# Eight modulation groups of the second block's odd layer are summed up on VectorE under the first feed forward, and GpSimd spreads the reciprocals of the attentions

## The reference

```python
x = x + concat(y_diff, y_moba) @ w_out[i]
x = x + conv_ffn(rms_norm(x, ln_ffn_g[i]), w_up[i], conv_w[i], conv_b[i], w_down[i])
```

```python
for i in range(2):
    ml = split(silu(c) @ w_ada[i] + b_ada[i], 6)        # latents
    mc = split(silu(c_ctx) @ w_ada[i] + b_ada[i], 6)    # context
    u_lat = rms_norm(h_lat, g_pre_mix[i]) * (1 + ml[1]) + ml[0]     # u_ctx likewise with mc
    o_lat, o_ctx = mixer(u_lat, u_ctx)                  # o_ctx in layer 0 only
    h_lat = h_lat + ml[2] * rms_norm(o_lat, g_post_mix[i])
    f_lat = square(relu(modulate(h_lat, g_pre_ff[i], ml[3], ml[4]) @ w_ff1[i])) @ w_ff2[i]
    h_lat = h_lat + ml[5] * rms_norm(f_lat, g_post_ff[i])
return h_lat
```

## Time and profile before

| | |
|---|---|
| median of three runs | 1936.65 us |
| profiled execution | 1936.78 us, span 1934.9 us |
| TensorE busy (matmul) | 1869.8 us, 97% |
| VectorE busy | 1105.8 us, 57% |
| ScalarE busy | 861.6 us, 45% |
| GpSimd busy | 211.9 us, 11% |
| bytes moved by DMA | 264.68 MB, 137 GB/s |

### The profile page before, as it was taken

The page is one execution under the profiler, slowest core; times in us unless marked ns, Lnnn a source line. Parts: engine busy times, 40 slices in busy tenths (PEclk is TensorE's granted clock), DMA queues, the critical chain, the costliest instruction groups (busy, mean ns, idle before and its releaser), DMA issues. The chain is left out here.

```text
span 1934.9 us, 37112 instructions
## 1 busy us (share of the span) xinstructions
PE 1869.8 (97%) x15824; PEld 1559.3 (81%) x15824; DVE 1105.8 (57%) x1835; ACT 861.6 (45%) x1559; POOL 211.9 (11%) x249
## 2 busy tenths in 40 slices
PE   7999999999999999999999999999999999899998
PEld 5768998776899788756898888888887798579986
DVE  6566774566667554476557665444444565546643
ACT  5465653446656542465322335322222254655532
POOL 2101221110122100103122211000000011000000
PEclk9999999999999999999999999999999999899999
DMA  7777665467766541353000042333332234024653
GB/s 267 250 256 224 189 183 175 166 227 263 223 166 195 175 142 55 115 174 110 26 4 4 4 151 65 104 119 98 100 107 88 66 99 139 25 88 133 194 180 124
DMA packets 219354, 264.68 MB, mean 137 GB/s; under 512 B 14214, under 2 KB 153782, under 8 KB 214711
## 3 DMA queue, kind: packets, MB, share of 16 engines
q1 hardware_dynamic: 218603, 261.49, 42.4%
q10 hardware_dynamic: 588, 0.82, 0.1%
HBM read 261.20 MB, written 1.09 MB: 136 GB/s over the span
## 5 line engine op out<-in xcount | busy, mean ns | idle before, releaser
L404 PE MATMUL acc<-rounded,rounded 128*128 128x512 f32 (+1 forms) x2552 | 875.1, 343 | 9.6 <-DVE rounded L684 4.1
L405 PE MATMUL acc<-rounded,rounded 128*128 128x512 f32 (+1 forms) x2552 | 867.0, 340 | 0.0
L406 PE MATMUL acc<-rounded,rounded 128*128 128x512 f32 (+1 forms) x2552 | 866.8, 340 | 0.0
L388 DVE TENSOR_TENSOR rounded<-arena,rounded 128x2048 fp32r<-128x2048 f32 (+1 forms) x194 | 434.3, 2241 | 285.9 <-ACT rounded L377 285.8
L404 PEld LDWEIGHTS acc<-rounded,rounded 128*128 128x128 f32 x2552 | 480.6, 188 | 80.1 <-issue 14.7
L405 PEld LDWEIGHTS acc<-rounded,rounded 128*128 128x128 f32 x2552 | 480.7, 188 | 60.0 <-issue 1.9
L406 PEld LDWEIGHTS acc<-rounded,rounded 128*128 128x128 f32 x2552 | 480.5, 188 | 60.0
L377 ACT ACTIVATE rounded<-arena 128x2048 fp32r<-128x2048 f32 (+1 forms) x194 | 362.9, 1873 | 341.6 <-PE acc L406 296.4
L1624 DVE SCALAR_TENSOR_TENSOR arena<-acc,pcol,arena 128x254 f32<-128x254 f32 (+1 forms) x176 | 76.8, 478 | 52.3 <-ACT arena L1605 50.8
L2200 PE MATMUL sc<-arena 64*64 64x64 f32 x2560 | 94.7, 221 | 8.8 <-DVE arena L2350 7.7
L2764 ACT ACTIVATE arena<-acc 128x512 f32<-128x512 f32 (+1 forms) x64 | 31.4, 490 | 159.6 <-PE acc L406 159.6
(11 more groups left out here) (265 smaller groups left out, 1691.6 us busy)
## 6 DMA issues: line engine op xcount, KB each, us to landing
arena<-in_w_ff SPq DMA_DIRECT2D x64, 1024.0 KB, 5.4
arena<-in_w_ada SPq DMA_DIRECT2D x48, 1024.0 KB, 5.1
arena<-in_w_up SPq DMA_DIRECT2D x88, 512.0 KB, 5.1
arena<-in_w_in SPq DMA_DIRECT2D x24, 1024.0 KB, 5.3
arena<-in_w_down SPq DMA_DIRECT2D x20, 1024.0 KB, 5.0
arena<-in_w_out SPq DMA_DIRECT2D x16, 1024.0 KB, 5.1
arena<-in_w_in_even SPq DMA_DIRECT2D x9, 1024.0 KB, 5.3
arena<-in_w_in_odd SPq DMA_DIRECT2D x8, 1024.0 KB, 5.2
```

The lines of the kernel that those rows point to most:

```text
L388: dve.tensor_tensor(r32(w), w, r32(high_slot(c)[:, 0:size(c)]), ALU.subtract).then_inc(split_made, 1)
L404: pe.matmul(ps, ah, bh, start=first, stop=False)
L405: pe.matmul(ps, ah, bl, start=False, stop=False)
L406: return pe.matmul(ps, al, bh, start=False, stop=last)
```

## The change

The eight groups leave the two attentions. Their 16 chunks stand in the list ahead of each `ff1(e)` and each `ff2(e)` (`plan_late`), so that the order in the first feed forward is one added chunk, two product chunks, one added chunk, and so on. `late_dve`, called ahead of the split of the chunk two positions on, adds up the 128x512 parts of an added chunk on VectorE, each multiplied by its column of silu(c), into `late_sum`; `late_pe` adds over the partitions by four matmuls with ones in the middle of the next `ff1` (the last one in the last round of `ff2`), and `late_add` adds the bias. The gains and gates of the odd layer follow at the start of `proj1` instead of scan step 0, except the gain of its first norm, and are transposed and stored apart from those of layer 0.

In the 48 units "by feature", GpSimd writes the broadcast reciprocals to SBUF (`widen`), and TensorE turns them by one transpose in place of the two matmuls. In `attBc` GpSimd's eight products stand between the units' copies.

Definitions that go away are shown by their first line (their text stands above). Not shown are the places of the new buffers, `ada_gains` (layer 0 alone now), the gates' loads and the calls of `widen` in the other attentions.

```diff
                 release.append((acc_full, acc_at[key] + i + 1))
-        ada_chunk = {}
-        def plan_ada(blocks, fill_of):
...
+        late_read = sem("late_read")
+        late_chunk = []
+        def plan_late():
+            n = len(late_chunk)
+            view = I["w_ada_2"][1].rearrange("(k p) n -> p k n", p=P)
+            c, k0 = 512 * (4 + n // 2), 4 * (n % 2)
+            late_chunk.append(len(chunks))
+            whole.add(len(chunks))
+            chunks.append(view[:, k0:k0 + 4, c:c + 512])
+            release.append((late_read, n + 1))
+            if n % 2:
+                stage(("late", n // 2), tr=1)
         def is_up(g):
...
                 c = split_chunks[n]
+                late_dve(dve, c)
                 dve.wait_ge(high_made, n + 1)
...
         stage("qT", tr=4)
-        stage("attBl", acc=16, tr=16 + 4, sc=8 + 4)
-        plan_ada(range(16, 20), lambda n: sc_at["attBl"] + 3 * n)
-        stage("attBc", acc=16, tr=8 + 4 + 8, sc=8 + 4)
-        plan_ada(range(20, 24), lambda n: sc_at["attBc"] + 3 * n)
+        stage("attBl", acc=16, tr=16, sc=8)
+        stage("attBc", acc=16, tr=8 + 8, sc=8)
         for s in range(NCH):
...
         def plan_ff1(e):
+            plan_late()
             stage(("ff1", e), acc=ET)
         def plan_ff2(e):
+            plan_late()
             stage(("ff2", e), acc=8)
...
         plan_norm(("mix", 1, 0))
+        stage("late_gates", tr=1)
         stage("proj1", acc=4 + 4 + 4 + 2 + 4, tr=6)
...
                         ins.then_inc(acc_full, 1)
-        def feat_gemm(pe, key, f, n, rhs, start=0):
+        def feat_gemm(pe, key, f, n, rhs, start=0, late=None):
             for i in range(start, n):
+                if i == 2 and late is not None:
+                    late_pe(pe, late)
                 if i % 2 == 0:
...
                                   start=(kb == 0), stop=(kb == n - 1), tile_position=(0, m * HD))
-                pe.wait_ge(att_comb, self.base + u + 1)
-                for m in range(2):
-                    ins = pe.matmul(ps[m * HD:(m + 1) * HD, P:2 * P], self.recip[:, 2 * u + m:2 * u + m + 1].broadcast_to([P, HD]), ident,
-                                    start=True, stop=True, tile_position=(0, m * HD))
+                i = self.featured.index(u)
+                pe.wait_ge(att_wide, self.spread_units + i + 1)
+                ins = pe.transpose(ps[:, P:2 * P], self.wide[:, i % 2, :], ident)
                 ins.then_inc(POOLS[self.values_at(u)[0]][1], 1)
                 for u in range(self.n):
-                    if self.ada:
-                        ada_pe(pe, self, u // 2, u % 2)
                     if self.group is not None and u % 2 == 0:
...
                         self.values(pe, u - 1)
-                    if self.ada and u and u % 2 == 0:
-                        ada_turn(pe, self, u // 2 - 1)
                     self.turn(pe, u)
                         hook(u)
-                if self.ada:
-                    ada_turn(pe, self, len(self.ada) - 1)
                 self.values(pe, self.n - 1)
...
                 ins.then_inc(drain(*f), 1)
+            def widen(self, pool, before=None):
+                for i, u in enumerate(self.featured):
+                    if before and u in before:
+                        before[u]()
+                    pool.wait_ge(att_comb, self.base + u + 1)
+                    if i >= 2:
+                        pool.wait_ge(att_spread, self.spread_units + i - 1)
+                    pool.tensor_copy(self.wide[:, i % 2, :].rearrange("p (m e) -> p m e", m=2),
+                                     self.recip[:, 2 * u:2 * u + 2].unsqueeze(2).broadcast_to([P, 2, HD])).then_inc(att_wide, 1)
             def outputs_by_feature(self, dve, u):
...
         mod_ready = sem("mod_ready")
-        mod_gates = mod_gate.rearrange("p l w k s -> p (l w k s)")
-        def ada_pe(pe, att, i, n):
...
-        def ada_act(act, att, i):
...
-        def ada_turn(pe, att, i):
...
+        gates_of = [mod_gate[:, l].rearrange("p w k s -> p (w k s)") for l in range(DEPTH)]
+        late_done = [0]
+        def late_dve(dve, c):
+            while late_done[0] < len(late_chunk) and late_chunk[late_done[0]] + 2 <= c:
+                n = late_done[0]
+                late_done[0] += 1
+                if n and n % 2 == 0:
+                    late_add(dve, n // 2 - 1)
+                g = late_chunk[n]
+                wait_landed(dve, g)
+                if n % 2:
+                    dve.wait_ge(late_read, n)
+                w = shaped(raw_slot(g), g)
+                for k in range(4):
+                    s = silu_c[:, 4 * (n % 2) + k, 0:1]
+                    if n % 2 == 0 and k == 0:
+                        ins = dve.tensor_scalar(late_sum, w[:, k, :], s, None, ALU.mult)
+                    else:
+                        ins = dve.scalar_tensor_tensor(late_sum, w[:, k, :], s, late_sum, ALU.mult, ALU.add)
+                    if k < 3:
+                        link(dve, ins)
+                ins.then_inc(late_read, 1)
+        def late_pe(pe, b):
+            pe.wait_ge(late_read, 2 * b + 2)
+            ps = claim(pe, "tr", tr_at[("late", b)])
             for n in range(4):
-                ins = pe.matmul(ps[:, 2 * n:2 * n + 2], mod_row[:, n * P:(n + 1) * P], const("quarter_sum"), start=True, stop=True)
+                ins = pe.matmul(ps[:, 2 * n:2 * n + 2], late_sum[:, n * P:(n + 1) * P], ones[:, 0:2], start=True, stop=True)
             ins.then_inc(tr_full, 1)
-        def ada_dve(dve, att, i):
...
+        def late_add(dve, b):
+            f = tr_at[("late", b)]
+            ps = filled(dve, "tr", f)
+            dve.tensor_tensor(mod[:, 1, 16 + 4 * b:20 + 4 * b, :], ps[:, 0:8].rearrange("p (a b) -> p a b", a=4),
+                              col("b_ada_2", 6 * KT + 16 + 4 * b, 4).unsqueeze(2).broadcast_to([P, 4, 2]), ALU.add)\
+               .then_inc(drain("tr", f), 1)
         WIDE = 4 * 512
...
                .then_inc(drain("tr", f), 1)
-        def ada_gains(dve, f, l):
...
+        def late_gains(dve):
+            wait_drained(dve, "tr", tr_at[("late", 7)])
+            pre_gain(dve, 1, 1)
+            for w in range(2):
+                post_gate(dve, 1, w).then_inc(mod_ready, 1)
         QK = {0: 0, 1: 1, 3: 2, 4: 3}
...
             pool.wait_ge(prep_done, 8)
-            for d in range(2):
-                for j in range(4):
-                    wait_drained(pool, "tr", att.more[3 if d else j])
-                    pool.tensor_tensor(kka[d][:, j, :], kk[:, j, :], rates[d][:, j, :], ALU.mult).then_inc(kka_done, 1)
+            def key_rates(*pairs):
+                def place():
+                    for d, j in pairs:
+                        wait_drained(pool, "tr", att.more[3 if d else j])
+                        pool.tensor_tensor(kka[d][:, j, :], kk[:, j, :], rates[d][:, j, :], ALU.mult).then_inc(kka_done, 1)
+                return place
+            att.widen(pool, {1: key_rates((0, 0)), 2: key_rates((0, 1)), 3: key_rates((0, 2)), 4: key_rates((0, 3), (1, 0)),
+                             5: key_rates((1, 1), (1, 2)), 6: key_rates((1, 3))})
             for d in range(2):
...
                 yTB_dve(dve, LATS)
-                ada_gains(dve, att_bc.ada_tr[-1], 1)
+                wait_drained(dve, "tr", tr_at[("group_turn", 3)])
+                pre_gain(dve, 1, 0).then_inc(mod_ready, 1)
             for lev in range(1, LEVELS):
...
                         near_pe(pe, 1, n)
+                    if n == 2:
+                        late_pe(pe, EIGHTHS - 1)
                     if n == 7:
...
                 elif e < EIGHTHS:
-                    feat_gemm(pe, ("ff1", e), acc_at[("ff1", e)], ET, lambda kt: both(uT, lambda v: v[:, kt, :]))
+                    feat_gemm(pe, ("ff1", e), acc_at[("ff1", e)], ET, lambda kt: both(uT, lambda v: v[:, kt, :]), late=e - 1)
                 if e:
...
                     dve.tensor_tensor(o, o, filled(dve, "acc", f)[:, :], ALU.add).then_inc(drain("acc", f), 1)
+                    if n == 3:
+                        late_add(dve, EIGHTHS - 1)
                     if n == 4:
...
             feat_gemm_by_stream(pe, "proj1_k", PK, 4, lambda s: ("mix", 1, s), {2: [0], 3: [1]})
+            pe.wait_ge(mod_ready, 5)
+            pe.transpose(claim(pe, "tr", tr_at["late_gates"])[0:2 * KT * 2, 0:P], gates_of[1], ident).then_inc(tr_full, 1)
             feat_gemm(pe, "proj1", PQ, 4, lambda kt: both(uT, lambda v: v[:, kt, SEQ:S2]))
...
             link(dve, dve.memset(no_near, 0.0))
+            late_gains(dve)
             for key in ("proj1_k", "proj1"):
...
                 qkv_pool(pool, l)
-                subnorm_pool(pool, l)
+                pool_att1(pool, l)
                 norm_pool(pool, ("ffn", l))
             kk_pool(pool)
+            att_bl.widen(pool)
             prep_pool(pool, att_bc)
```

(59 more changed lines are left out.)

79 lines of the change are left out of this document (41 added, 38 removed).

## The result

| | before | after |
|---|---|---|
| median | 1937.18 us (4 runs, 1934.16 to 1938.49) | 1951.45 us (4 runs, 1950.59 to 1953.15) |
| ratio | | 1.0077, interval 1.0059 to 1.0094 |
| profiled execution | 1936.78 us, span 1934.9 | 1951.19 us, span 1949.4 |
| TensorE busy | 1869.8 us, 97% | 1855.8 us, 95% |

The kernel became 14.3 us slower. The forecast was slower by 6.6, 1943.4 us, with a range up to 1950, so the sign was right and the size was not: the time lies outside the range.

What follows compares the result with a forecast made beforehand. TensorE, busy 97% of the span, was taken as the bound. Terms −13.6 − 6.2 + 7.4 + 8.9 + 7.2 + 3.4 − 0.5 = +6.6 us gave 1943.4 us; 8-in-10 range 1931 to 1950.

Steps and rivals of the forecast that it cites:

- The groups that leave the attentions: Latents' and context's attention: shorter loops per unit win 4.1 and 9.5 us, together −13.6, from −8 to −20.
- The transposes: First blocks and odd block: one transpose for two spreading products saves 0.19 us in each of 32 units, −6.2 us.
- Rival D: GpSimd's copies hold VectorE up or come late behind the key products: up to +4.8, 1948 us; chance 0.09.
- The column sums: First feed forward: eight calls of four products by ones cost TensorE 0.92 us each, +7.4 us, bounds 4 and 8.
- The hidden part: First feed forward: VectorE's 46 us of sums and the 16 added chunks lie beside TensorE's work, costed at 0.
- The two look-ahead stops: TensorE waits for late splits at the feed forward's start, +8.9 us, and the odd block's projection, +7.2 us.
- Clock: Behind the two new stalls: one stretch of lower granted clock each, +3.4 us, bounds 0 and 7.
- The scan: Scan step 0: one gain operation in place of four on VectorE, −0.5 us.

Runs made afterwards that it cites:

- both_splits: Changed kernel with ff1(0)'s second chunk split ahead of the latents' norm and proj1_k's first chunk split in ff2's last round: 1934.39 us, 0.9996 of the kernel before.
- spread_first: Kernel before, with GpSimd's spreading and the transpose in the first block's 16 units alone: 1936.98 us, 1.0006.
- both_one_op: Changed kernel with both early splits and one VectorE operation in place of four per added chunk: 1933.55 us, 0.9993 of the kernel before.
- start_split: Changed kernel with the second chunk of ff1(0) split ahead of the latents' norm: 1946.23 us, 1.0054 of the kernel before.
- end_split: Changed kernel with the first chunk of proj1_k split in the last round of ff2: 1944.43 us, 1.0042 of the kernel before.
- (5): Changed kernel with both early splits plus overwritten filler matmuls on TensorE in the even attentions: 1933.42 us, with more fillers 1943.75, with fewer 1931.90.
- both_filled_less: Changed kernel with both early splits and the fewest overwritten filler matmuls tried in the even attentions: 1931.90 us, 0.9978 of the kernel before.
- (8): Kernel before with GpSimd's spreading and the transpose in the second block's 32 units (1934.64, repeated 1935.98 us), the first's 16 (1936.98) or all 48 (1932.84).

## Why the prediction was wrong

**1. The groups that leave the attentions: right.** −13.9 against −13.6. The loops came out as worked out, 3.84 and 2.84 us a unit. In the changed kernel's latents TensorE waits 3.3 us for ScalarE's exponentials and 4.1 for its copies; before it waited 1.3 for the exponentials, and no wait of the value products for the copies is in the list. In the executions with more low-clock stretches the gain is less: in both_splits' trace the two attentions gave 10.0 us instead of 13.9.

**2. The transposes: wrong.** This is the step that failed most: it priced each of 32 units at 0.19 us, 6.2 us in all, and 1.7 came. The price took the 0.32 us from the first spreading product to the transposes of the probabilities for the cost of the pair, and 0.13 us for a transpose among transposes as the cost of its replacement. One unit of the first block, before and after (value products, spreading, transposes):

```profile
116.38 0.44 PE L899 MATMUL sc<-arena 128*64 128x128 f32 x4
116.64 0.39 PE L903 MATMUL sc<-keep,stat 128*64 128x128 f32 x4
116.96 0.66 PE L876 MATMUL tr<-keep,arena 128*128 128x128 f32 x4
```

```profile
116.52 0.44 PE L894 MATMUL sc<-arena 128*64 128x128 f32 x4
116.89 0.33 PE L898 MATMUL sc<-keep,arena 128*128 128x128 f32 x1
117.05 0.60 PE L871 MATMUL tr<-keep,arena 128*128 128x128 f32 x4
```

The pair started 0.26 us behind the start of the value products, the transpose starts 0.37 behind it. The weights of the pair were being loaded 0.10 us ahead of it, under the value products (116.54); those of the transpose are loaded when it starts (116.89). So 0.11 us of the saving are spent ahead of the transpose. From the value products to the product behind the transposes it was 1.17 us and is 1.06: a unit saves 0.11, not 0.19.

In the first block, where the step took TensorE for the full engine, even that is taken back in every second unit, where the next value products wait for ScalarE's copy, before and after the change. The shift falls by 0.3 us in each layer in spread_first. In the changed kernel's trace it does so in layer 1 alone; in layer 0 TensorE waited 0.50 us for a chunk of modulation weights. In C and D the shift falls by 0.11 us from unit to unit, 1.5 in all. Another 1.6 us that it falls by there are not the transposes': the kernel before had a stretch at the lower clock from 1686 us (0.72 over 1685 to 1691), the changed one has none there. A longer one at the start of C took 1.5 back.

No matmul waited for GpSimd's copies, as forecast; two weight loads of the transposes did, 0.3 us together. Rival D named the right operation and the wrong cause: VectorE's 128x2 sum in the context's attention takes 642 ns in the mean now and took 428.

```profile
L940 DVE TENSOR_TENSOR stat<-stat,neg_sink 128x2 f32<-128x2 f32 x8 | 5.1, 642 | 0.3
```

That is eight times 0.2 us, 1.7 us of VectorE's time in a stretch that got 10 us shorter all the same. But the sums that took 0.67 to 1.20 us run beside the 128x512 products of GpSimd (L2102) and end with one of them; none runs beside a copy, and the two that run beside nothing took 0.16.

**3. The column sums: right**, 0.87 us for each eighth, 7.0 us against 7.4 in the sum.

**4. The hidden part: nearly right.** 1.2 us were not hidden, in the relative-position products of one round, where VectorE came 0.95 us late; both_one_op took them away. The two look-ahead stops were right in place, cause and size, 8.4 and 9.3 us of idle time against 8.9 and 7.2 us that the sum has for them, and start_split and end_split removed them.

**5. Clock: right in kind behind the stops.** Around the second, from 1566.4 us on, the clock was low for 10.24 us, and the two stops with their clock cost 19.2 us against 19.5. What the step left out is the clock in the attentions that the change empties; in this trace it cost nothing (0.98 before and after), in others it did (5).

**6. The scan: wrong.** Forecast −0.5, measured +2.3 there and 0.3 in the output projection. Waits that the profile ascribes to nothing account for 1.6 of it (0.95 and 0.69 us); the rest is in small waits that I did not trace. In both_filled_less, with the same work in the scan, it was 0.4 us with the output projection, and the 0.95 us are not there. The step had no term for such waits. Why they come stays open: late instructions fit all traces (8), and nothing was run that shows it.

So of the 7.8 us that the sum was short, 4.5 stand in the stages of step 2 (3.0 and 1.5), 3.1 in the scan's, and the rest is what the other stages miss by, 0.2 together. That the stage of C and D shows the transposes' own 1.6 us is luck: the clock gave as much there as it took. The range was too narrow for a sum of seven terms of which three had no row for their cover.

## What to carry to other kernels

A look-ahead that counts positions in a list loses depth when entries that don't use it are put into the list: count the entries that do, and look at the first and the last of them. A busy share of 95% doesn't make an engine the bound; ask what its next instruction waits for once this one is shorter. What an instruction costs between its neighbours is read from the start of the one before it to the start of the one behind it, for the old form and for the new one in the same neighbourhood. Work taken from TensorE in a stage with waits may come back as clock, and gains of one part in a thousand must be checked for waits that have no cause in the program.

## What the runs showed of the hardware

The idle time ascribed to "issue" in the scan's second step was 0 to 2.18 us, depending on the kernel, though TensorE's instructions there are the same, and it was longest where the instruction queue's packets paused longest; at 2.18 us it cost with its clock some 4 us. Two parts of a change that each measure as nothing (1.0006 and 0.9997) measured as 0.9980 together, and in the traces the difference lies in the scan, where these waits are.

A transpose of 128x128 behind products whose weights are 128x64 started 0.20 us after the last of them (116.68 to 116.89), where a product with 128x64 weights had started after 0.10 us (116.54 to 116.64).

Removing 10 us of matmuls from a 90 us stretch left its granted clock at 0.98 in one execution and put it at 0.85 to 0.94 in five others. With overwritten matmuls it was 0.96 to 1.00, and the median of all runs went from 0.9996 to 0.9978 of the kernel before, though on different chips, with intervals that overlap, and with other waits in the scan.
